# The SSD layer's in-chunk product of both directions as one product of the unscaled x, its decay matrix formed one pair ahead

## The chip, the cores and the metric

The kernel runs on one core of a Trainium2 chip. The metric is the time of the program on the device in microseconds (us), the median of the runs; lower is better. TensorE (PE) multiplies matrices, VectorE (DVE), ScalarE (ACT) and GpSimd (POOL) do elementwise work, SyncE (SP) issues the DMAs.

## The reference, cut to what matters

Two token groups (256 and 512 tokens, 768 in all) pass two layers with shared weights. Layer 0 is a bidirectional Mamba-2 SSD mixer with 32 heads of 64, in chunks of 128 tokens, layer 1 a neighbourhood attention. The change touches the SSD mixer only:

```python
def ssd_chunked(x, a_dt, bm, cm):
    ...
    decay_ls = jnp.exp(jnp.where(lower, seg, -jnp.inf))
    cb = jnp.einsum('bclgn,bcsgn->bcgls', cm, bm)
    y_diag = jnp.einsum('bcgrls,bcsgrp->bclgrp', cb[:, :, :, None] * decay_ls, x)
    ...
    return (y_diag + y_off).reshape(b, t, SSD_HEADS, p)

def ssd_direction(xs, bm, cm, dt_raw, dt_bias, a_log):
    dt = jax.nn.softplus(dt_raw.astype(jnp.float32) + dt_bias.astype(jnp.float32))
    ...
    return ssd_chunked(xs * dt[..., None].astype(xs.dtype), a_dt, bm, cm)
...
    y_fwd = ssd_direction(xs, bm, cm, dt_f, dt_bias_f, a_log_f)
    y_bwd = flip(ssd_direction(flip(xs), flip(bm), flip(cm), flip(dt_b), dt_bias_b, a_log_b))
    y = (y_fwd + y_bwd + d_skip[:, None] * xs)
```

So inside a chunk y is (C B masked to one triangle, times the decay) times (x dt_f), plus the same with the other triangle times (x dt_b). All is float32.

## The kernel before

Every engine has its own instruction list, written out by hand; semaphores order them. An engine runs its list strictly in order, so a wait holds up all that stands behind it.

`ssd_phase` goes through 16 pairs of heads (n = 0 to 15), for all 768 tokens (6 chunks of 128) at once. In pair n PE does, in this order:

- a dense unit, the input projection of x for pair n+1 (`pe_dense`, 24 products with 256 columns, then 24 with 512); between these two halves `turn_x` (L1791) transposes x of pair n;
- the chunk states (L1820), which need x scaled (`x_scaled`) and write over the banks A[2], A[3] in which the transposed x lay;
- the sums of squares of pair n-1 (L1797), in pairs 3, 7, 11 also the transposes for the next group of B (L1772);
- the dense unit of z for pair n; in "group pairs" 1, 5, 9 two more dense units, the next B and C;
- in pairs 3, 7, 11 C B of the next group (L1781);
- in even pairs from 2 on ("out pairs") two units of the output projection (`pe_out`, L264), 12 tiles, each of which DVE adds to `acc` (L298, copies at L296 in pair 2);
- the y block (L1850, L1854): per chunk two products for each direction with the in-chunk decay matrices `dec` and `seg` (L1850), and those with the carried states (L1854). It waits for `gated` of pair n-1, `carried`, `dec_ready` and `cs_ready`.

DVE in pair n: `scale_x` (L1631, from the turned x four products: with the two state weights and with dt_f and dt_b), in pairs 0, 4, 8, 12 the masked C B (L1649: `cb_u`, `cb_l`), the segment sums (L1656, L1659), the low part of the mix (L1618), C times the decays (L1674), then `dec` and `seg` from the exponentials and `cb_u`, `cb_l` (L1684, L1685), the carries (L1692), the convolution of x for pair n+1 (four taps, L1262; in out pairs they stand between the output tiles, the last one behind tile 10 of 12; in group pairs the taps of B and C follow), then waits for `y_done` and does y (L1732) and the gate (L1735).

ACT in pair n: exponentials (L1528, with a table load), the take of x for pair n+1 (L1200, L1201), the exponentials of the segments (`decay`, L1537, twelve of 128x128), the copies of the states (L1551 to L1553), the take of z (L245, L246), SiLU of the convolved x for pair n+1 (L1210, behind `conv_done`; in group pairs that of C comes last), then, behind `gated`, the square (L1573) and the high part of the mix (L1586), and so on with pair n+1.

POOL splits every weight unit in two (L188, L191). The names the change touches: `xx`/`xdt`/`xw`, `wt` (0, 1: state weights; 2, 3: dt_f, dt_b), `dec`, `seg`, `cb_u`, `cb_l`, `dec_ready`, `x_scaled`, `cb_taken`.

Of the kernel before, what the change touches and what calls it, by code (L numbers as in the profile page):

```python
# [14 lines left out]
P = 128  # L15
# [3 lines left out]
T = NP_ + NS  # L19
# [61 lines left out]
def encoder_kernel(nc, x_prompt, x_sample, mem_prompt, mem_sample, pre_g, post_g, mem_g, w_mem_kv, w_out,  # L81
# [3 lines left out]
    with ctx:  # L85
# [5 lines left out]
        def sem(name):  # L91
            return ctx.enter_context(nc.semaphore(name))
# [482 lines left out]
        def memory_phase(phase, L, pre=None, place=None, ssd=None):  # L575
# [32 lines left out]
            if L:  # L608
                with ExitStack() as after:
# [12 lines left out]
                sem(n + x) for x in ("post_gain_landed", "summed", "added", "post_sums", "post_root", "post_scaled",  # L622
                                     "x1_stored"))
            macc_landed, res_landed = ([sem(f"{n}{x}{i}") for i in range(2)] for x in ("macc_landed", "res_landed"))
# [472 lines left out]
        class Prelude:  # L1097
# [9 lines left out]
            def window(self, r):  # L1107

                at, r.at = r.at, 0
                self.ab, self.cs, self.xx = r(2, 2, T), r(2, 2, 4, P), r(4, NT, P)  # L1110
# [270 lines left out]
        def ssd_phase(phase, pre, nxt, mixes):  # L1381
            w_in = ssd_w_in[0]
            ab, cs, xx = pre.ab, pre.cs, pre.xx
            xw, xdt = xx[:, 0:2, :, :], xx[:, 2:4, :, :]
# [17 lines left out]
             expanded) = (  # L1402
# [3 lines left out]
                    "sq_done", "sq_summed", "summed", "reduced", "rooted", "expanded"))  # L1406
# [49 lines left out]
            def sync(sp):  # L1456
# [35 lines left out]
                sp.wait_ge(x_scaled, PAIRS)  # L1492
                nxt.load_mem(sp, 3)
# [10 lines left out]
            def scalar(act):  # L1504
                take_raw, silu = pre.takes(act)
                def take_bt(g):

                    act.wait_ge(bt_turned, g + 1)
                    if g:
                        act.wait_ge(states_done, 4 * g)  # L1510
                    act.activation(btok[:, 0:2, :], A[5][:, 0:NP_].rearrange("p (c l) -> p c l", l=P), ACT.Copy)
                    act.activation(btok[:, 2:6, :], A[4][:, :].rearrange("p (c l) -> p c l", l=P), ACT.Copy)\
                        .then_inc(bt_taken, 1)

# [3 lines left out]
                for n in range(PAIRS):  # L1518
# [23 lines left out]
                    if n < LAST:  # L1542
                        take_raw(j, n + 1)
# [54 lines left out]
            def vector(dve):  # L1598
# [13 lines left out]
                def both_heads(t):  # L1612
                    return t.unsqueeze(2).broadcast_to(shape)

# [8 lines left out]

                for n in range(PAIRS):
                    g, a = n // 4, n % 2
                    def scale_x():
                        dve.wait_ge(x_turned, n + 1)
                        for q, (c0, c1) in enumerate(((0, 2), (2, 6))):
                            ch = slice(2 * c0, 2 * c1)
                            pieces = [P, 4, 2 * (c1 - c0), 64]  # L1630
                            i = dve.tensor_tensor(  # L1631
                                xx.rearrange("p k c (h f) -> p k (c h) f", h=2)[:, :, ch, :],
                                A[2 + q][:, 0:(c1 - c0) * P].rearrange("p (c f) -> p c f", f=64).unsqueeze(1)
                                .broadcast_to(pieces),
                                wt[:, :, n, ch].unsqueeze(3).broadcast_to(pieces), ALU.mult)
# [7 lines left out]
                    if n % 4 == 0:  # L1643
# [8 lines left out]
                        dve.wait_ge(cb_taken, g + 1)  # L1652

# [28 lines left out]

                    dve.wait_ge(seg_exp, n + 1)
# [79 lines left out]
            def tensor(pe):  # L1763
                def chunk(bank2, ch):
                    return bank2[ch > 1][:, (ch if ch < 2 else ch - 2) * P:][:, 0:P]
# [37 lines left out]
                for n in range(PAIRS):  # L1803
# [12 lines left out]
                    pe.wait_ge(x_scaled, n + 1)  # L1816
                    pe.wait_ge(bt_taken, g + 1)
# [568 lines left out]
```

## Time and profile before

| | us |
|---|---|
| median of 3 runs | 2189.82 (2189.72 to 2192.56) |
| span of the profiled execution | 2187.1 |
| PE busy | 2125.7 (97%) |
| DVE busy | 1086.6 (50%) |
| ACT busy | 712.5 (33%) |
| POOL busy | 930.9 (43%) |

The span of the profiled execution is its own time as the profiler sees it; the median of the runs is 2.7 us above it. Columns of a page line and of a group of instructions: line and engine, operation, out<-in, count, then busy us and mean ns of one, then the idle time before them and what ended it. The SSD pairs run from 411 to 992 us of the span. Busy shares are of time in which at least one instruction was under way; a PE that is busy may still wait inside its pipeline.

### The profile page before, as it was taken

To read this page: it belongs to the slowest core of one execution; us is meant where nothing else is said; L and a number is where in the kernel's file an instruction comes from. 1 tells how busy PE (TensorE), PEld (TensorE's weight loads), DVE (VectorE), ACT (ScalarE), POOL (GpSimd) and SP (SyncE) were. 2 spreads that over 40 slices of the span, in tenths; PEclk is the share of its full clock that TensorE was granted. 3 is DMA by queue.
4 is the path that set the end of the run, shared out by engine and by line. 5 is a ranking of instruction groups with operands and counts; after the bars stand their busy time and mean duration, and the time that the engine had idled before them with its cause. 6 is when DMAs were issued, how large, how long until landed. Compare 5 with 4: busy or idle time off the path is not lost.

```text
span 2187.1 us, 31495 instructions
## 1 busy us (share of the span) xinstructions
PE 2125.7 (97%) x12986; PEld 1817.9 (83%) x12986; DVE 1086.6 (50%) x1685; ACT 712.5 (33%) x1618; POOL 930.9 (43%) x623
## 2 busy tenths in 40 slices
PE   7999999999999999999999999999999999999997
PEld 6888887888888888887788887888888888888885
DVE  4103333688888888897711333144323423541436
ACT  4123122344353344443322121043323323432243
POOL 4533333232443442334743333655454445554534
PEclk9999999999999999999999999999999999999999
DMA  6221212344322232334441111322231223122212
GB/s 193 87 70 51 53 55 81 116 105 113 97 94 80 78 106 78 96 106 155 136 135 49 49 58 39 104 85 62 62 87 57 67 57 94 43 64 85 66 49 116
DMA packets 206666, 184.72 MB, mean 84 GB/s; under 512 B 23899, under 2 KB 172667, under 8 KB 206523
## 3 DMA queue, kind: packets, MB, share of 16 engines
q1 hardware_dynamic: 206523, 182.72, 27.2%
q8 instruction: 102, 1.67, 0.3%
q14 instruction: 41, 0.34, 0.1%
HBM read 168.71 MB, written 12.21 MB: 83 GB/s over the span
## 4 chain that ended last, share of the span: by engine, by line
PE 49%; DVE 4%; issue 1%; ACT 1%; DMA 0%; POOL 0%; DVEq 0%; POOLq 0%
PE bank L214 24%; PE bank L264 9%; PE bank L567 6%; PE bank L2288 2%; PE bank L2259 2%; PE bank L2271 2%; PE bank L1000 2%; PE bank L1026 1%; DVE acc L911 1%; PE bank L1064 1%; DVE acc L915 1%; DVE acc L905 0%; PE bank L440 0%; DVE R L2148 0%; PE bank L2328 0%
## 5 line engine op out<-in xcount | busy, mean ns | idle before, releaser
L188 POOL TENSOR_SCALAR Wh<-Wraw 128x1024 fp32r<-128x1024 f32 x217 | 252.3, 1163 | 1137.9 <-issue 765.5
L214 PE MATMUL bank<-Hh,Wh 128*128 128x512 f32 (+1 forms) x1936 | 664.9, 343 | 6.3 <-ACT R L1201 3.6
L214 PE MATMUL bank<-Hl,Wh 128*128 128x512 f32 (+1 forms) x1936 | 652.2, 337 | 0.0
L214 PE MATMUL bank<-Hh,Wl 128*128 128x512 f32 (+1 forms) x1936 | 651.2, 336 | 0.0
L191 POOL TENSOR_TENSOR Wl<-Wraw,Wh 128x1024 fp32r<-128x1024 f32 x217 | 550.2, 2535 | 18.1
L214 PEld LDWEIGHTS bank<-Hh,Wh 128*128 128x128 f32 x1936 | 367.5, 190 | 54.8 <-issue 14.3
L214 PEld LDWEIGHTS bank<-Hh,Wl 128*128 128x128 f32 x1936 | 367.1, 190 | 38.9
L214 PEld LDWEIGHTS bank<-Hl,Wh 128*128 128x128 f32 x1936 | 367.7, 190 | 36.5 <-issue 1.7
L298 DVE TENSOR_TENSOR acc<-bank,acc 128x512 f32<-128x512 f32 x240 | 164.9, 691 | 170.6 <-PE bank L264 169.7
L264 PE MATMUL bank<-Wh,Mh 128*128 128x512 f32 x528 | 209.3, 396 | 11.3 <-DVE acc L298 11.3
L264 PE MATMUL bank<-Wh,Ml 128*128 128x512 f32 x528 | 206.5, 391 | 0.0
L264 PE MATMUL bank<-Wl,Mh 128*128 128x512 f32 x528 | 206.5, 391 | 0.0
L2025 POOL TENSOR_TENSOR R<-R 128x160 f32<-128x160 f32 (+2 forms) x160 | 109.1, 720 | 84.1 <-DVE R L2184 84.0
L1262 DVE SCALAR_TENSOR_TENSOR R<-R 128x770 f32<-128x770 f32 x96 | 135.8, 1420 | 13.2 <-ACT R L1201 11.7
L264 PEld LDWEIGHTS bank<-Wh,Mh 128*128 128x128 f32 x528 | 99.5, 189 | 38.9 <-DVE acc L298 17.2
L2157 DVE TENSOR_TENSOR R<-bank,R 128x256 f32<-128x256 f32 (+1 forms) x32 | 24.3, 837 | 206.5 <-PE bank L2288 206.5
L2148 DVE TENSOR_SCALAR R<-R 128x256 f32<-128x256 f32 (+2 forms) x192 | 126.2, 723 | 1.1
L931 DVE TENSOR_REDUCE R<-bank 128x2 f32<-128x512 f32 x24 | 16.6, 692 | 214.5 <-PE bank L1026 214.5
L2178 DVE CUSTOM_DVE_ANT_0 R<-bank,R 128x160 f32<-128x160 f32 (+2 forms) x192 | 57.9, 365 | 127.6 <-PE bank L2259 127.3
L264 PEld LDWEIGHTS bank<-Wl,Mh 128*128 128x128 f32 x528 | 99.6, 189 | 21.2
L264 PEld LDWEIGHTS bank<-Wh,Ml 128*128 128x128 f32 x528 | 99.5, 188 | 19.7
L246 ACT ACTIVATE R<-bank 128x512 f32<-128x512 f32 x62 | 37.1, 598 | 218.4 <-PE bank L214 218.4
(238 smaller groups left out, 3067.2 us busy)
## 6 DMA issues: line engine op xcount, KB each, us to landing
Wraw<-in_na_w_in_dram SPq DMA_DIRECT2D x80, 512.0 KB, 3.7
Wraw<-in_ssd_w_in_dram SPq DMA_DIRECT2D x57, 512.0 KB, 4.2
Wraw<-in_w_out_dram SPq DMA_DIRECT2D x48, 512.0 KB, 3.3
R<-acs_dram SPq DMA_DIRECT2D x16, 1536.0 KB, 6.2
Wraw<-in_w_mem_kv_dram SPq DMA_DIRECT2D x32, 512.0 KB, 3.7
R<-gs_dram SPq DMA_DIRECT2D x32, 128.0 KB, 3.5
macc_dram<-acc SPq DMA_DIRECT2D x1, 3072.0 KB, 9.1
R<-macc_dram SPq DMA_DIRECT2D x6, 512.0 KB, 4.2
```

Source lines behind the costliest of these rows:

```text
L188: pool.tensor_scalar(Wh[:, s, :], Wraw[:, s, :], 1.0, 1.0, ALU.mult, ALU.mult).then_inc(pool_c, 1)
L191: pool.tensor_tensor(Wl[:, s, :], Wraw[:, s, :], Wh[:, s, :].bitcast(F32), ALU.subtract)\
L214: mm = pe.matmul(DB[h.k % 2][:, 0:t1 - t0], w[:, k, :], x[:, k, t0:t1], start=(k == 0 and i == 0), stop=(k == KC - 1 and i == 2))
L264: mm = pe.matmul(A[4 + o.k % 2][:, :], x[k][:, i * P:(i + 1) * P], w[:, k, :], start=(k == 0 and j == 0), stop=(k == 1 and j == 2))
L298: dve.tensor_tensor(dst, A[4 + o.k % 2][:, :], dst, ALU.add).then_inc(out_added, 1)
L567: mm = pe.matmul(self.banks[t][:, :], x[:, 2 * j + k, tok], y[:, k, :], start=(j == 0 and k == 0 and p == 0), stop=(j == 3 and k == 1 and ...
L1000: mm = pe.matmul(V_BANK[t][:, :], x[:, 2 * j + k, tok], y[:, k, :], start=(j == 0 and k == 0 and p == 0), stop=(j == 3 and k == 1 and p == 2))
L1262: i = dve.scalar_tensor_tensor(o, x[:, k:k + w], self.cw[:, m + 24 * k:m + 24 * k + 1], o, ALU.mult, ALU.add)
L2025: i = pool.tensor_tensor(o, m, src, ALU.add)
L2148: i = dve.tensor_scalar(s, s, rinv[:, o, h:h + 1], None, ALU.mult)
L2178: i = dve.tensor_tensor_reduce(Sb[:, h, S_AT[b]:S_AT[b] + w], A[3 * h + bk][:, c0:c0 + w], Bm[:, h, m:m + w], 1.0, -3e38, ALU.add, ALU.max ...
L2259: mm = pe.matmul(A[3 * h + bk][:, c0:c0 + w], qF[f, q0:q0 + P], kF[f, k0:k0 + w], start=True, stop=True)
```

## The change

Since both in-chunk products of a head are summed, they can be one: with E the exponential of the segments, y = sum over s of x times E times (cb_u dt_f + cb_l dt_b). The new kernel

- forms that bracket M for pair n+1 at the end of pair n. ACT (`forward`) writes `dec` = cb_u * dt_f, twelve copies of 128x128 with a scale of one number per partition, behind its last SiLU of the pair and ahead of `gated`; DVE (`backward`) adds cb_l * dt_b with twelve scalar_tensor_tensor of 128x128, behind the last tap and ahead of `y_done`. Those of pair 0 stand in pair 0, ahead of `decay` and of the product with E;
- makes one product of E and M on DVE (`seg`) where there were two (L1684, L1685);
- halves the products of L1850 on PE: x unscaled (`xtok`) times `seg`, two per chunk instead of four;
- has DVE scale x with two weights instead of four (L1631), and ACT copy the unscaled x from PSUM (`copy_x`, 256 and 512 columns), behind `x_scaled` and between the two halves of the take of x for pair n+1; PE's states (L1820) wait for this copy too (`x_copied`);
- moves the masked C B of groups 1 to 3 from the start of pairs 4, 8, 12 to the end of pairs 3, 7, 11, ahead of `backward`;
- leaves out seven semaphores in layer 0 to have three new ones.

```diff
+                def copy_x(n):
+                    act.wait_ge(x_scaled, n + 1)
+                    for q, (c0, c1) in enumerate(((0, 2), (2, 6))):
+                        i = act.activation(xtok[:, c0:c1, :], A[2 + q][:, 0:(c1 - c0) * P]
+                                           .rearrange("p (c f) -> p c f", f=P), ACT.Copy)
+                    i.then_inc(x_copied, 1)
+
+                def forward(n):
+                    if n % 4 == 0:
+                        act.wait_ge(cb_taken, n // 4 + 1)
+                    if n:
+                        act.wait_ge(dec_ready, n)
+                    for ch in range(NT):
+                        for h in range(2):
+                            i = act.activation(dec[:, ch, h, :], cb_u[:, ch, :], ACT.Copy,
+                                               scale=wt[:, 2, n, 2 * ch + h:2 * ch + h + 1])
+                    i.then_inc(dec_forward, 1)
...
                     if n < LAST:
-                        take_raw(j, n + 1)
+                        take_raw(j, n + 1, lambda: copy_x(n))
+                    else:
+                        copy_x(n)
+                    if n == 0:
+                        forward(0)
                     decay()
...
                     elif n < LAST:
                         silu(j, n + 1, xs[1 - a])
+                    if n < LAST:
+                        forward(n + 1)
...
+                def backward(n):
+                    dve.wait_ge(dec_forward, n + 1)
+                    for ch in range(NT):
+                        for h in range(2):
+                            i = dve.scalar_tensor_tensor(dec[:, ch, h, :], cb_l[:, ch, :],
+                                                         wt[:, 3, n, 2 * ch + h:2 * ch + h + 1], dec[:, ch, h, :],
+                                                         ALU.mult, ALU.add)
+                    i.then_inc(dec_both, 1)
...
-                            pieces = [P, 4, 2 * (c1 - c0), 64]
+                            pieces = [P, 2, 2 * (c1 - c0), 64]
...
+                    if n == 0:
+                        backward(0)
                     dve.wait_ge(seg_exp, n + 1)
-                    c.add(dve.tensor_tensor(dec, seg, both_heads(cb_u), ALU.mult))
-                    dve.tensor_tensor(seg, seg, both_heads(cb_l), ALU.mult).then_inc(dec_ready, 1)
+                    dve.wait_ge(dec_both, n + 1)
+                    dve.tensor_tensor(seg, seg, dec, ALU.mult).then_inc(dec_ready, 1)
...
+                    if next_group(n):
+                        take_cb(g + 1)
+                    if n < LAST:
+                        backward(n + 1)
 
                     dve.wait_ge(y_done, n + 1)
...
                     pe.wait_ge(x_scaled, n + 1)
+                    pe.wait_ge(x_copied, n + 1)
...
-                        for d, weight in enumerate((dec, seg)):
-                            for h in range(2):
-                                pe.matmul(chunk(A[0:2], ch)[H64[h], :], xdt[:, d, ch, H64[h]], weight[:, ch, h, :],
-                                          start=(d == 0), stop=False)
+                        for h in range(2):
+                            pe.matmul(chunk(A[0:2], ch)[H64[h], :], xtok[:, ch, H64[h]], seg[:, ch, h, :],
+                                      start=True, stop=False)
```

## Rows read from the trace of the kernel before

**Rows 1.** Page, part 1: each engine's busy us, share and instructions.
```profile
PE 2125.7 (97%) x12986; PEld 1817.9 (83%) x12986; DVE 1086.6 (50%) x1685; ACT 712.5 (33%) x1618; POOL 930.9 (43%) x623
```
**Rows 2.** Windows by pair: length, busy PE, PEld, DVE, ACT, POOL, clock, DMA.
```profile
527.30:554.40 27.10, 27.10 (x230) 24.88 (x228) 24.50 (x26) 14.19 (x32) 6.46 (x4) 1.00 0.36 115
...
sum 580.80, PE 564.73 PEld 497.80 DVE 488.12 ACT 253.60 POOL 211.63; mean PE 35.30 PEld 31.11 DVE 30.51 ACT 15.85 POOL 13.23
```
**Rows 3.** Timeline of PE, end of pair 4 to states of pair 5.
```profile
592.98 0.66 PE L1850 MATMUL bank<-R 128*64 128x128 f32 x8
...
597.18 0.39 PE L1854 MATMUL bank<-R 128*64 128x128 f32 x4
...
606.61 1.95 PE L1820 MATMUL bank<-R 128*128 128x128 f32 x16
```
**Rows 4.** Timeline of DVE, same stretch: start, us, instruction, [idle before <-releaser].
```profile
592.34 1.01 DVE L1262 SCALAR_TENSOR_TENSOR R<-R 128x770 f32<-128x770 f32 x1
...
597.61 1.27 DVE L1732 SCALAR_TENSOR_TENSOR R<-R,bank 128x256 f32<-128x256 f32 x2 [3.67 <-PE bank L1854]
```
**Rows 5.** Timeline of ACT, same stretch, and its exponentials of the segments.
```profile
593.38 1.12 ACT L1210 ACTIVATE R<-R 128x256 f32<-128x256 f32 x2 [17.61 <-DVE R L1262]
599.91 0.85 ACT L1573 ACTIVATE R<-R 128x768 f32<-128x768 f32 x1 [5.40 <-DVE R L1735]
...
604.99 0.36 ACT L1200 ACTIVATE R<-bank 128x256 f32<-128x256 f32 x1
605.25 0.46 ACT L1201 ACTIVATE R<-bank,R 128x256 f32<-128x256 f32 x1
606.81 0.60 ACT L1200 ACTIVATE R<-bank 128x512 f32<-128x512 f32 x1 [1.10 <-PE bank L214]
...
610.37 3.63 ACT L1537 ACTIVATE R<-R 128x128 f32<-128x128 f32 x12 [2.38 <-DVE R L1659]
```
**Rows 6.** Timeline of DVE in pair 3: the removed forms, the nearest small ones.
```profile
539.30 2.49 DVE L1674 TENSOR_TENSOR R<-R 128x256 f32<-128x256 f32 x4
...
543.15 1.76 DVE L1684 TENSOR_TENSOR R<-R 128x1536 f32<-128x1536 f32 x1 [0.42 <-ACT R L1537]
...
546.50 1.75 DVE L1692 SCALAR_TENSOR_TENSOR R<-R,bank 128x64 f32<-128x64 f32 x8
```
**Rows 7.** Groups of DVE by form: the scaling of x, its two sizes.
```profile
L1631 DVE TENSOR_TENSOR R<-bank,R 128x2048 f32<-128x2048 f32 x16 | 36.5, 2280 | 0.0
L1631 DVE TENSOR_TENSOR R<-bank,R 128x1024 f32<-128x1024 f32 x16 | 19.6, 1223 | 12.1 <-PE bank L1791 11.9
```
**Rows 8.** Group pair 5, timelines: PE's y block starts; ACT's last SiLU.
```profile
636.26 0.66 PE L1850 MATMUL bank<-R 128*64 128x128 f32 x8
...
636.86 1.11 ACT L1210 ACTIVATE R<-R 128x256 f32<-128x256 f32 x2
```
**Rows 9.** Pair 3, timelines of DVE and PE: last taps, y, y block.
```profile
548.15 6.21 DVE L1262 SCALAR_TENSOR_TENSOR R<-R 128x770 f32<-128x770 f32 x3
554.53 1.26 DVE L1732 SCALAR_TENSOR_TENSOR R<-R,bank 128x256 f32<-128x256 f32 x2 [0.16 <-PE bank L1854]
...
549.89 0.66 PE L1850 MATMUL bank<-R 128*64 128x128 f32 x8
```
**Rows 10.** First pairs, timelines of PE and DVE: waits, the taps of x.
```profile
433.28 0.93 PE L1850 MATMUL bank<-R 128*64 128x128 f32 x8 [2.19 <-DVE R L1692]
...
451.06 2.05 PE L1820 MATMUL bank<-R 128*128 128x128 f32 x16 [0.95 <-DVE R L1631]
...
433.14 9.41 DVE L1262 SCALAR_TENSOR_TENSOR R<-R 128x770 f32<-128x770 f32 x4
```
**Rows 11.** Windows behind PE's wait of pair 0; the clock is third from last.
```profile
433.30:437.00 3.70, 3.70 (x38) 3.70 (x40) 3.67 (x2) 0.00 (x0) 3.62 (x3) 0.54 0.07 16
437.00:439.80 2.80, 2.80 (x48) 2.63 (x45) 2.73 (x3) 0.00 (x0) 2.72 (x2) 1.00 0.50 138
```
**Rows 12.** Waits of PE, whole span: us in total, times, longest.
```profile
PE bank L264 <- DVE acc L298: 13.4, 9, 2.8
```

More of the change, by code:

```diff
@@ L621, in memory_phase @@
             post_gain_landed, summed, added, post_sums, post_root, post_scaled, x1_stored = (
-                sem(n + x) for x in ("post_gain_landed", "summed", "added", "post_sums", "post_root", "post_scaled",
-                                     "x1_stored"))
-            macc_landed, res_landed = ([sem(f"{n}{x}{i}") for i in range(2)] for x in ("macc_landed", "res_landed"))
+                sem(n + x) if L else None for x in ("post_gain_landed", "summed", "added", "post_sums", "post_root",
+                                                    "post_scaled", "x1_stored"))
+            macc_landed, res_landed = ([sem(f"{n}{x}{i}") for i in range(2)] if L else None
+                                       for x in ("macc_landed", "res_landed"))
             where = InOrder() if L == 0 else ByColumn()
@@ L1109, in window @@
                 at, r.at = r.at, 0
-                self.ab, self.cs, self.xx = r(2, 2, T), r(2, 2, 4, P), r(4, NT, P)
+                self.ab, self.cs, self.xx = r(2, 2, T), r(2, 2, 4, P), r(3, NT, P)
                 r.at = at
@@ L1383, in ssd_phase @@
             ab, cs, xx = pre.ab, pre.cs, pre.xx
-            xw, xdt = xx[:, 0:2, :, :], xx[:, 2:4, :, :]
+            xw, xtok = xx[:, 0:2, :, :], xx[:, 2, :, :]
             raw, conv, bT, acs_tok, tot_tok, wt, cw, dcol, ssum = (
@@ L1401, in ssd_phase @@
              ab_exp, dec_ready, cs_ready, y_done, gated, hi_ready, sq_done, sq_summed, summed, reduced, rooted,
-             expanded) = (
+             expanded, x_copied, dec_forward, dec_both) = (
                 sem("g_" + x) for x in (
@@ L1405, in ssd_phase @@
                     "seg_ready", "seg_exp", "ab_exp", "dec_ready", "cs_ready", "y_done", "gated", "hi_ready",
-                    "sq_done", "sq_summed", "summed", "reduced", "rooted", "expanded"))
+                    "sq_done", "sq_summed", "summed", "reduced", "rooted", "expanded", "x_copied", "dec_forward",
+                    "dec_both"))
             F_DST, B_DST = (1, 3, 4, 5), (0, 2, 3, 4)
@@ L1492, in sync @@
                 sp.wait_ge(x_scaled, PAIRS)
+                sp.wait_ge(dec_both, PAIRS)
                 nxt.load_mem(sp, 3)
@@ L1629, in scale_x @@
                             ch = slice(2 * c0, 2 * c1)
-                            pieces = [P, 4, 2 * (c1 - c0), 64]
+                            pieces = [P, 2, 2 * (c1 - c0), 64]
                             i = dve.tensor_tensor(
-                                xx.rearrange("p k c (h f) -> p k (c h) f", h=2)[:, :, ch, :],
+                                xw.rearrange("p k c (h f) -> p k (c h) f", h=2)[:, :, ch, :],
                                 A[2 + q][:, 0:(c1 - c0) * P].rearrange("p (c f) -> p c f", f=64).unsqueeze(1)
                                 .broadcast_to(pieces),
-                                wt[:, :, n, ch].unsqueeze(3).broadcast_to(pieces), ALU.mult)
+                                wt[:, 0:2, n, ch].unsqueeze(3).broadcast_to(pieces), ALU.mult)
                             if q:
@@ L1642, in vector, with take_cb @@
                         scale_x()
-                    if n % 4 == 0:
+                    def take_cb(g):
                         dve.wait_ge(bc_done, g + 1)
@@ L1652, in vector @@
                         dve.wait_ge(cb_taken, g + 1)
+                    if n == 0:
+                        take_cb(0)
                     def segment():
@@ L1681, in vector @@
                         conv5(j, n + 1, dense, (0,))
+                    if n == 0:
+                        backward(0)
                     dve.wait_ge(seg_exp, n + 1)
-                    c.add(dve.tensor_tensor(dec, seg, both_heads(cb_u), ALU.mult))
-                    dve.tensor_tensor(seg, seg, both_heads(cb_l), ALU.mult).then_inc(dec_ready, 1)
+                    dve.wait_ge(dec_both, n + 1)
+                    dve.tensor_tensor(seg, seg, dec, ALU.mult).then_inc(dec_ready, 1)
                     dve.wait_ge(prev_set, n + 1)
```

2 lines of the change are left out of this document (removed).

## The prediction

> **What bounds the kernel now.** I read the page first: PE is busy 97% of the span [rows 1]. So a gain has to come out of PE's list, and a loss has to be a wait that PE doesn't have today. Next I read windows cut at the ends of the y blocks, one for each of the 16 pairs. Over all of them, 580.8 us, PE is busy 564.7, so it waits 16.1 us; in pair 3 it doesn't wait at all (27.1 of 27.1 us), with DVE busy for 24.5 [rows 2]. The reader is to see that DVE has little room in such a pair, and that the page's 50% for DVE is a mean over stages and says nothing of this one. Then I read the timelines of PE, DVE and ACT for one stretch, from the y block of pair 4 to the states of pair 5 [rows 3 to 5], since the change puts new work just where these three hand over to each other. The result is worked out there.
>
> **What PE gives up.** The y block of pair 4 starts at 592.98 and DVE takes y from 597.61; the last matmul group starts at 597.18 [rows 3, 4]. That is 4.5 us for 80 records (48 of L1850, two for each product, and 32 of L1854), in one unbroken stream. Half of L1850 goes, 24 records, 24/80 x 4.5 = 1.35 us. For 16 pairs that is **-21.6 us**. If the stream were bound by something other than its records it would be less, not under 0.
>
> **Where the new work stands.** I count from the start of the y block of pair 4 (592.98 = 0). DVE's last tap of the convolution ends at 593.35, +0.4 [rows 4]; ACT's SiLU, two instructions, ends at 594.50, +1.5 [rows 5]. Today both are then idle: DVE 3.67 us until y_done, ACT 5.40 us until the gate [rows 4, 5]. The change fills this with a chain, not with parallel work: `forward` stands behind SiLU on ACT, `backward` waits for it on DVE, and DVE's y and gate stand behind `backward`.
>
> - `forward`: twelve ACT instructions of 128x128 with one number per partition. The twelve exponentials of the segments have the same count, size and such an operand: 3.63 us [rows 5]. It ends at +5.2.
> - `backward`: twelve DVE instructions of 128x128, from no row directly. Upper bound: the eight carries (same operation, 64 columns) take 1.75 us, 0.21 each start to start; 64 more columns at about 1.1 ns (1.76 us for 1536 columns) give 0.28, so 3.4 us. Lower bound: the four products L1674 take 2.49 us for 2048 columns, which leaves 0.06 each beyond the columns, so 0.20 and 2.4 us [rows 6]. I take 2.9, the middle: the first has the same operation, the second all operands in SBUF as here. It ends at +8.1.
>
> The y block now ends at +3.2 (4.55 - 1.35), but DVE begins y at +8.1: **4.9 us after y_done** where it was at once.
>
> **What hangs on it.** PE doesn't wait for the gate of the last pair soon, but for the states it does, through x. Behind DVE's y (597.61) come the gate, ACT's square (599.91), the high part, the table load, the exponentials and the first half of the take of x, whose last instruction ends at 605.71 and lets the next one start some 0.1 earlier [rows 4, 5]. There `copy_x` now stands, 256 and 512 columns, 0.27 + 0.60 = 0.87 us by the takes L1200 [rows 5]: 8.9 us after DVE began y. PE wants to start the states 9.0 us after y_done (597.61 to 606.61) [rows 3, 4]. So the new wait `x_copied` alone would have been free by 0.1 us, and for just that reason all of the 4.9 us falls on PE: a wait of 4.8 us in the pair behind. PE has no other work in its list to put before it. Its cover, were it gone by another 1 us (ACT busy at the take), costs 1 us more in each pair.
>
> SP's next load of the segment sums waits for ACT's exponentials and for L1659, and the weights queue behind it; these come later by the same delay as PE does, so I put nothing on the weights. SP's last new wait, `dec_both`, is met long before.
>
> **The sum of the new waits.**
> - Behind out pairs (2, 4, ... 14): 7 x 4.8 = 33.6.
> - Behind group pairs (1, 5, 9): the chain starts with SiLU of C, which ends at 637.97, +1.7 [rows 8]; + 3.7 + 2.9 = +8.3, 5.1 after y_done; less the 0.1, 3 x 5.0 = 15.0.
> - Behind pairs 3, 7, 11, 13: here DVE's taps are the last thing. They ended at 554.36, 4.5 after the y block's start [rows 9]. DVE enters pair 3 4.9 late, PE 4.8 late; DVE saves half of the scaling, (2.28 + 1.22)/2 = 1.75 [rows 7], and one product of 1.76 [rows 6], 3.5 in all. So the taps end at +1.1. Then the masked C B, moved to here, 2 us by the L1674 row (three times ahead of `forward`), `forward` and `backward` to +9.7, 6.5 after y_done. That is 6.4 behind the 0.1 of cover for three of them and 4.4 to 5 for pair 13; DVE and POOL slow each other in places, which varies these. I take 6 x 4 = 24.
> - Behind pair 0: taps of x took 9.41 us and end at 442.55 [rows 10]. + 1.1 + 3.7 + 2.9, then the same 8.9: `x_copied` at 459.2, where the states started at 451.06 [rows 10]: 8.
> - In pair 0 `forward` stands ahead of the exponentials, on the path to the carries for which PE waits 2.19 us today [rows 10]: +3.6 on ACT, -3.5 on DVE and an overlap with PE's dense unit. I put 0, bounds -2 and +3.6.
>
> Together **+80.6 us**.
>
> **What goes with it.** Of PE's 16.1 us of waits today [rows 2], some lie where DVE or ACT was a little late: at the output tiles (13.4 us in the whole span, at nine places [rows 12]), at the states and at the takes. The new wait stands ahead of them in the same pair and takes their place. I put **-10**, bounds 0 and -14. The moved mask and shorter DVE list act only here.
>
> **The clock.** PE waited 2.19 us in pair 0, and then the granted clock was 0.54 for 3.7 us (1.2 GHz for most of it) and 1.00 after it [rows 10, 11]: 1.7 us lost. Each of the 15 new waits is longer than that one. Behind the waits of even pairs DVE and ACT don't set the next delay, PE's output tiles do, so the loss stays; before the others DVE is last and hides it. 7 x 1.7 = 12, bounds 0 and 15 x 1.7 = 26; I take **+10**. The Trainium skill ("TensorE: Matmul & The Clock Gate", "HAM oscillation") says that a wait that comes back in every trip of a loop pays the change of the clock each time; the row on pair 0 agrees for one wait. By that rule the sum would have the 26 in place of the 10.
>
> The Trainium skill ("VectorE: DVE Perf Modes", on the TRN2 errata) also speaks against this change: many small instructions from SBUF pay a fixed latency each, which one large one pays once. The rows show it mildly: twelve pieces are priced at 2.9 us here and the one product they stand for took 1.76. Its measured fixed term of about 150 cycles would make `backward` an estimated 3.5 us, and the sum some 9 us more.
>
> **Forecast.** -21.6 + 80.6 - 10 + 10 = **+59 us** on the span, 2187.1 to 2246. The median stands 2.7 above the span: 2189.8 + 59 = **2249 us**, 2.7% slower.
>
> **The rivals.**
> 1. *Half the chain is hidden.* If PE's states were released some 2.5 us earlier than I read (the takes and exponentials packed closer once they start late, or a `backward` under its bound), each of the 15 waits would be 2.5 shorter and the clock would mostly stay: 59 - 37 - 8 = +14, 2204. Against it: from y to the first take ACT has no idle gap to squeeze [rows 5]. 0.08.
> 2. *Faster, the other side.* PE's saving is kept whole if `backward` ends by y_done, that is if the chain behind the tap takes under 2.8 us (3.2 - 0.4) in place of 7.7. Then waits at the tiles shrink too: -21.6 - 3 = -25, 2165. For it: PE is the bound, and both DVE and ACT are idle just where the work is put. Against it: `forward` alone is 3.6 by its nearest row. 0.05.
> 3. *The clock falls each time and stays down longer.* If each wait costs 1.7 us of clock and more on the path (say 3, on all 15) and `backward` is at its upper bound (+0.5 each): 59 - 10 + 45 + 8 = +102, 2292. For it: the waits are twice as long as the one seen. Against it: DVE is last in every second pair and doesn't feel PE's clock. 0.12.
> 4. *The gain and the waits cancel* (within 4.4 us of before): needs the chain to be 3.4 us or so shorter; nothing points there. 0.02.
>
> The forecast has 0.73. Bounds inside it: `backward` 2.4 to 3.4 (-8, +8), the pairs 3, 7, 11, 13 from 5 to 7 each (-4, +4), clock -10 to +16, old waits -4 to +10, pair 0 +-3. These don't all go one way: -27 to +32, so 2222 to 2281; the 0.73 are nearly all in it. With a little of the third case the **range is 2220 to 2283**. A difference of 0.2% (4.4 us) is about what a measurement of this kernel tells from none. Faster 0.05, the same 0.02, slower 0.93.
>
> **What would show it.** In the profile after: y blocks of 3.2 us (right for the saving); PE's wait for L1820, released by ACT's copy from PSUM, 4 to 7 us in 15 pairs (right for the chain), with DVE idle between its last tap and the first small instruction for 4.5 to 5 us; a granted clock near 0.5 behind these waits. Wrong would be: PE waits only at y (then `dec` is last, not x), or `forward` found far from 3.6 us, or the states released by DVE rather than ACT, or no wait over 2 us in the out pairs.

## The result, and the profile after

The changed kernel takes 2291.97 us (median of 4 runs, 2288.70 to 2295.99) where the kernel before, run beside it, takes 2190.24: ratio 1.0463, 95% interval 1.0447 to 1.0479. That is 102 us slower; the prediction was 59 us slower, 2249, with a range up to 2283. The sign, the place and the length of the waits are as forecast; the price of TensorE's clock is not.

The page after: engines, and the granted clock in 40 slices of the span.

```profile
span 2291.9 us, 31139 instructions
...
PE 2163.0 (94%) x12602; PEld 1850.1 (81%) x12602; DVE 1063.3 (46%) x1861; ACT 780.2 (34%) x1842; POOL 919.3 (40%) x623
...
PEclk9999999988998899898999999999999999999999
```

PE has 384 records fewer than in [rows 1] (16 pairs x 24) and yet is busy 37 us longer. Fewer instructions and more busy time point to a slower clock, and slices 9 to 19, the SSD pairs, show it (before had 9 in every slice).

Windows cut at the ends of the y blocks (length, busy PE, PEld, DVE, ACT, POOL, clock, DMA), here pairs 1, 3 and 4:

```profile
438.70:498.50 59.80, 48.16 (x283) 42.77 (x283) 40.30 (x48) 27.36 (x65) 19.03 (x10) 0.83 0.34 88
...
549.80:584.70 34.90, 30.24 (x205) 27.69 (x206) 23.91 (x41) 18.90 (x46) 8.44 (x5) 0.85 0.28 91
...
584.70:632.70 48.00, 42.54 (x259) 36.50 (x259) 32.15 (x49) 19.32 (x49) 14.59 (x8) 0.93 0.24 77
```

Pair 3 was 27.10 us without a wait [rows 2]; it is 34.90 now, with PE idle for 4.66 and the rest a clock of 0.85. Over all 16 pairs the windows come to 682.20 us with PE busy 598.95, against 580.80 and 564.73 [rows 2]. So of the 101.4 us, **67.2 are idle PE** (83.25 in place of 16.07) **and 34.2 are busy PE**. Another 2.7 us lie ahead of the pairs, in work that the change doesn't touch, 0.7 behind them. The 2.7 are the clock of this execution: it was 0.51 from 16 to 23 us and 0.57 from 272 to 276 us, where the trace of before has 1.00. The traces of all thirteen runs start their first states at 419.1 to 423.5, whatever the kernel, and latest in the three in which the clock is down near 272 us.

The waits of PE in this stretch (us in total, times, longest):

```profile
PE bank L1864 <- issue: 63.9, 13, 5.5
PE bank L1864 <- DVE R L1665: 8.0, 1, 8.0
PE bank L1840 <- ACT R L1601: 6.1, 1, 6.1
PE bank L1834 <- ACT R L1211: 3.7, 1, 3.7
PE bank L1893 <- DVE R L1731: 1.6, 1, 1.6
```

L1864 are the states (L1820 before), which answer to [rows 3, 10]. There is one wait for each of pairs 1 to 14, as forecast; the one forecast for pair 15 stands at its sums of squares (L1840). "issue" says that the record names no releaser: the instruction waits for two semaphores. The timelines do name it. From the last tap of pair 4 to the states of pair 5, DVE and then ACT, the answer to [rows 4, 5]:

```profile
628.80 1.01 DVE L1263 SCALAR_TENSOR_TENSOR R<-R 128x770 f32<-128x770 f32 x1
...
634.52 3.24 DVE L1653 SCALAR_TENSOR_TENSOR R<-R 128x128 f32<-128x128 f32 x12 [4.10 <-ACT R L1533]
637.68 1.26 DVE L1775 SCALAR_TENSOR_TENSOR R<-R,bank 128x256 f32<-128x256 f32 x2
```
```profile
629.85 1.12 ACT L1211 ACTIVATE R<-R 128x256 f32<-128x256 f32 x2 [16.36 <-DVE R L1263]
630.88 3.61 ACT L1533 ACTIVATE R<-R 128x128 f32<-128x128 f32 x12
639.97 0.84 ACT L1601 ACTIVATE R<-R 128x768 f32<-128x768 f32 x1 [5.48 <-DVE R L1778]
...
645.67 0.87 ACT L1521 ACTIVATE R<-bank 128x256 f32<-128x256 f32 x2
```

Read them as one staircase: tap to 629.81, SiLU to 630.97, `forward` (L1533) to 634.49, `backward` (L1653) to 637.76, y, gate, square, exponentials, take, `copy_x` (L1521) to 646.54, and PE starts the states at 646.63. The y block had ended at 632.73; y starts 4.95 after it.

PE's states, some of the 15, with their idle time in brackets:

```profile
423.51 1.95 PE L1864 MATMUL bank<-R 128*128 128x128 f32 x16
461.35 3.75 PE L1864 MATMUL bank<-R 128*128 128x128 f32 x16 [7.96 <-DVE R L1665]
...
646.63 3.75 PE L1864 MATMUL bank<-R 128*128 128x128 f32 x16 [4.69 <-issue]
742.00 3.76 PE L1864 MATMUL bank<-R 128*128 128x128 f32 x16 [4.68 <-issue]
778.78 3.75 PE L1864 MATMUL bank<-R 128*128 128x128 f32 x16 [5.45 <-issue]
...
1012.61 3.60 PE L1864 MATMUL bank<-R 128*128 128x128 f32 x16 [4.68 <-issue]
```

The same 16 products take 1.95 us in pair 0 and 3.1 to 3.8 behind each wait. Windows behind the waits ahead of the states of pairs 3, 7 and 13, which were all of 4.66 to 4.68 us (length, busy PE, PEld, DVE, ACT, POOL, then the clock):

```profile
563.65:570.00 6.35, 6.35 (x30) 6.35 (x31) 5.95 (x7) 5.17 (x17) 0.00 (x0) 0.50 0.57 215
...
742.00:753.30 11.30, 11.30 (x53) 11.30 (x54) 10.80 (x18) 6.04 (x19) 1.45 (x1) 0.50 0.75 233
1012.61:1016.10 3.49, 3.49 (x18) 3.49 (x18) 3.49 (x5) 2.98 (x9) 0.00 (x0) 0.52 0.26 81
```

In the first PE is busy all 6.35 us at 1.2 GHz, so 3.2 us are lost there; the clock stays down until 572.4, and the whole stretch loses 4.4. In the second 5.6 are lost and in the third 1.7, though the waits ahead of them were equal. Over all 16 places it is 1.6 to 6.0 us each, 58 in all. In [rows 11] the clock was 0.54 for 3.7 us.

### The profile page after: what moved, and what is told of

Read it like the earlier page. It is cut to its first block, busy times and chain, and to the rows that moved or that the text cites. A ratio compares the mean times of both kernels' runs of the same rounds, so it can differ in the third digit from the quotient of the medians.

```text
span 2291.9 us, 31139 instructions
## 1 busy us (share of the span) xinstructions
PE 2163.0 (94%) x12602; PEld 1850.1 (81%) x12602; DVE 1063.3 (46%) x1861; ACT 780.2 (34%) x1842; POOL 919.3 (40%) x623
## 4 chain that ended last, share of the span: by engine, by line
PE 83%; DVE 9%; ACT 4%; issue 3%; DMA 1%; POOL 0%; SPq 0%; DVEq 0%; POOLq 0%
PE bank L214 43%; PE bank L264 15%; PE bank L567 6%; PE bank L1001 4%; PE bank L1864 2%; ACT R L1533 2%; PE bank L2314 2%; PE bank L2331 2%; PE bank L1027 2%; PE bank L2302 2%; DVE R L1653 1%; PE bank L1840 1%; PE bank L1065 1%; DVE R L1665 1%; PE bank L440 1%
## 5 line engine op out<-in xcount | busy, mean ns | idle before, releaser
L188 POOL TENSOR_SCALAR Wh<-Wraw 128x1024 fp32r<-128x1024 f32 x217 | 242.6, 1118 | 1254.4 <-issue 889.9
L214 PE MATMUL bank<-Hh,Wh 128*128 128x512 f32 (+1 forms) x1936 | 673.6, 348 | 2.6 <-ACT R L793 1.4
L214 PE MATMUL bank<-Hl,Wh 128*128 128x512 f32 (+1 forms) x1936 | 660.1, 341 | 0.0
L214 PE MATMUL bank<-Hh,Wl 128*128 128x512 f32 (+1 forms) x1936 | 657.9, 340 | 0.0
L191 POOL TENSOR_TENSOR Wl<-Wraw,Wh 128x1024 fp32r<-128x1024 f32 x217 | 548.4, 2527 | 18.1
L214 PEld LDWEIGHTS bank<-Hh,Wh 128*128 128x128 f32 x1936 | 375.9, 194 | 50.7 <-issue 9.9
L214 PEld LDWEIGHTS bank<-Hh,Wl 128*128 128x128 f32 x1936 | 374.8, 194 | 39.6
L214 PEld LDWEIGHTS bank<-Hl,Wh 128*128 128x128 f32 x1936 | 375.8, 194 | 36.8 <-issue 1.7
L1263 DVE SCALAR_TENSOR_TENSOR R<-R 128x770 f32<-128x770 f32 x96 | 124.0, 1291 | 31.4 <-ACT R L1202 29.9
L1864 PE MATMUL bank<-R 128*128 128x128 f32 x256 | 55.3, 404 | 71.8 <-issue 63.9
```

The source lines that it names most:

```text
L188: pool.tensor_scalar(Wh[:, s, :], Wraw[:, s, :], 1.0, 1.0, ALU.mult, ALU.mult).then_inc(pool_c, 1)
L191: pool.tensor_tensor(Wl[:, s, :], Wraw[:, s, :], Wh[:, s, :].bitcast(F32), ALU.subtract)\
L214: mm = pe.matmul(DB[h.k % 2][:, 0:t1 - t0], w[:, k, :], x[:, k, t0:t1], start=(k == 0 and i == 0), stop=(k == KC - 1 and i == 2))
L1263: i = dve.scalar_tensor_tensor(o, x[:, k:k + w], self.cw[:, m + 24 * k:m + 24 * k + 1], o, ALU.mult, ALU.add)
L1864: mm = pe.matmul(A[2 + d][:, s * P:(s + 1) * P], btok[:, src[s], :], xw[:, d, src[s], :], start=True, stop=True)
```

## The experiments

All times are medians beside runs of the kernel before on the same chip (2189.7 to 2190.4). "After" is the changed kernel.

### Is it the clock? Other products in the waits

**e5_warm_first** puts products that nobody reads into PE's list ahead of both waits:

```diff
+                    if n:
+                        pe.wait_ge(gated, n)
+                        for _ in range(34 if n == 1 else 20):
+                            pe.matmul(A[1][:, :], Hh[:, 0, 0:P], Hh[:, 0, NP_:T], start=True, stop=True)
                     pe.wait_ge(x_scaled, n + 1)
                     pe.wait_ge(x_copied, n + 1)
```

> As e1_warm (the kernel after with products that nothing reads), but these stand ahead of both waits, for the scaled and for the copied x, and there are 34 of them in pair 1. In e1 PE sat 2.7 us idle for the scaled x before it came to them in every second pair, and then did 4.8 us of them, past the moment when x was there. Here they fill the idle time itself. Theory A (the clock costs some 50 us on top of the waits): 2236 to 2248. Theory B (it doesn't): 2285 to 2295.

Measured: 2250.84 us, ratio 1.0277 (1.0259 to 1.0296), 3 us above the range of theory A and far from theory B. The kernel is 41 us faster than after, with more work on PE. In its trace the states take 2.02 us wherever they come behind such products, with what is left of the waits:

```profile
751.09 2.02 PE L1868 MATMUL bank<-R 128*128 128x128 f32 x16 [0.92 <-issue]
...
994.71 2.02 PE L1868 MATMUL bank<-R 128*128 128x128 f32 x16 [1.28 <-issue]
```

So at least 41 of the 102 us are clock; the waits themselves are still paid, by products instead of idleness. Two waits have no such cover, and the clock still falls behind them: at `turn_x` in pair 1 (3.6) and at the sums of squares in pair 15 (6.1).

**e1_warm** has the same 20 products between the two waits, so PE stands idle for `x_scaled` first.

```diff
                     pe.wait_ge(x_scaled, n + 1)
+                    if n:
+                        pe.wait_ge(gated, n)
+                        for _ in range(20):
+                            pe.matmul(A[1][:, :], Hh[:, 0, 0:P], Hh[:, 0, NP_:T], start=True, stop=True)
                     pe.wait_ge(x_copied, n + 1)
```

> The kernel after, with 20 products of 128x512 that nothing reads (4.6 us at full clock) put on PE ahead of its wait for the copied x, in pairs 1 to 15. The waits there are 4.7 to 8 us, so the products lie inside them and only keep PE busy. Theory A (about 55 us of the 101 lost in the SSD pairs are the lower clock behind 15 waits, not the waits): the clock stays near 1.00, 2292 falls by 45 to 52 to 2240 to 2247, although PE has more work. Theory B (what comes on top of the waits is late data or shared ports, and the low clock only goes with it): no gain, 2290 to 2300.

Measured: 2275.16, ratio 1.0387 (1.0366 to 1.0408), between the two. The reason is in its waits and two of its blocks:

```profile
PE bank L1863 <- DVE R L1665: 24.4, 10, 6.4
```
```profile
552.75 6.42 PE L1863 MATMUL bank<-Hh 128*128 128x512 f32 x20 [2.73 <-DVE R L1665]
585.53 4.83 PE L1863 MATMUL bank<-Hh 128*128 128x512 f32 x20 [0.57 <-DVE R L1665]
```

In six pairs PE stands idle for 2.7 us first, and then the products run on past the time at which `x_copied` is given (`copy_x` ends at 554.61, the products at 559.17), so the chain gets longer. Behind five of the six waits the clock fell as well, so that the products themselves took 6.4 to 6.5 us in place of 4.83; behind the sixth, of 2.71, it stayed. The states come at the full clock (1.95 to 2.05 us) each time. The run mixes all this; e5 is the one that prices the clock.

### Is it where the new work stands? The same change without "a step ahead"

**e2_own_pair** keeps everything of the change (one product with the bracket, half of PE's in-chunk products, `copy_x`), but forms M of pair n in pair n: `forward` ahead of `decay`, `backward` ahead of the product, the masked C B back at pairs 4, 8, 12.

```diff
+            EARLY = ()
...
-                    if n == 0:
-                        forward(0)
+                    if n not in EARLY:
+                        forward(n)
                     decay()
...
-                    if n < LAST:
-                        forward(n + 1)
...
-                    if n == 0:
-                        take_cb(0)
+                    if n % 4 == 0:
+                        take_cb(g)
...
-                    if n == 0:
-                        backward(0)
+                    if n not in EARLY:
+                        backward(n)
                     dve.wait_ge(seg_exp, n + 1)
...
-                    if next_group(n):
-                        take_cb(g + 1)
-                    if n < LAST:
-                        backward(n + 1)
```

> The kernel after, but M of pair n is formed in pair n: ACT's twelve copies behind the take of x and ahead of the exponentials of the segments, DVE's twelve ahead of the product with E; the masked C B at the start of pairs 4, 8, 12 as before. The same instructions, only elsewhere. Theory A (it is the place, behind SiLU and ahead of the gate, that costs): no waits of 4 to 8 us are left, PE keeps its 21.6 us less some 4 for the wait on the copied x behind odd pairs: 2172 (2163 to 2182). Theory C (it is the load, 24 small instructions a pair on engines without room): DVE becomes last in pairs without output tiles, 2190 to 2210.

Measured: 2179.83 us, ratio 0.9956 (0.9940 to 0.9972); again on another chip:

> The same program as e2_own_pair, run again beside the two behind it so that the three share a chip. Expected: 2178 to 2182 us again, 0.4 to 0.5% under the kernel before.

Measured: 2179.89, ratio 0.9952 (0.9938 to 0.9965). So the change without the step ahead is a gain of 10 us, and the step ahead (M and the masked C B together) costs 112. Its waits of PE in the pairs (the second run):

```profile
PE bank L1888 <- DVE R L1730: 6.6, 2, 5.0
PE bank L1829 <- ACT R L1211: 6.3, 3, 3.7
PE bank L1859 <- issue: 5.0, 3, 1.9
PE bank L214 <- ACT R L1202: 3.2, 3, 1.3
PE bank L264 <- DVE acc L298: 2.8, 3, 1.4
```

The 14 long waits at the states are gone (three are left, at `copy_x`, 1.9 at most). One long one has come: 5.0 at the y block of pair 15.

**e10_last_forward** is e2_own_pair with something done about that one alone: `AHEAD` holds pair 15.

```diff
-                    if n not in EARLY:
+                    if n not in AHEAD:
                         forward(n)
                     decay()
...
                     act.activation(prev[:, 1, 3, :], A[3][:, 3 * P:4 * P], ACT.Copy).then_inc(prev_set, 1)
+                    if n + 1 in AHEAD:
+                        forward(n + 1)
```

> e2_own_pair with forward of the last pair alone issued one step ahead on ACT, behind the copies of the states of pair 14; backward and the product stay in pair 15. In e2_own_pair PE waits 5.0 us at the y block of pair 15 for DVE's carries. Theory (the wait comes from ACT doing forward, 3.6 us, in front of the exponentials of the segments there, with no other work to cover it): the wait falls to about 1.4 us, total 2175 to 2178. Rival (it comes from DVE's own additional work, backward 3.2 us less what was saved, so ACT's order does not matter): the wait stays at 4 to 5 us and the total within 1 us of e2_own_pair.

Measured: **2172.57 us**, ratio 0.9930 (0.9918 to 0.9943), 7.3 under e2b_own_pair (4.9 by the means, since two of the five runs of e10 are at 2177): more than expected. The y block of pair 15 and the clock behind its wait (third from last) in e2b_own_pair and then here:

```profile
977.34 0.69 PE L1888 MATMUL bank<-R 128*64 128x128 f32 x4 [5.00 <-DVE R L1730]
...
977.34:981.00 3.66, 3.66 (x37) 3.66 (x39) 2.02 (x3) 3.52 (x7) 1.26 (x2) 0.53 0.76 284
```
```profile
971.18 0.44 PE L1891 MATMUL bank<-R 128*64 128x128 f32 x4 [1.73 <-DVE R L1733]
...
971.18:975.00 3.82, 3.82 (x59) 3.55 (x60) 2.47 (x4) 3.67 (x6) 0.18 (x1) 1.00 1.00 340
```

The wait is 3.3 us shorter, and the clock that fell behind the long one (1.7 us lost) stays up behind the short one: 5.0 us together. The two traces are 7.9 us apart, but of that 2.2 lie ahead of the pairs, which the edit doesn't touch, so the rest of the 7.3 can't be put down to this wait. With e11, below, this is the fastest kernel of this study.

**e11_odd_forward** is the same with `AHEAD` holding the pairs 1, 3, 5, 7, 9, 11, 13, 14 and 15.

> e2_own_pair with forward issued one step ahead on ACT, behind the copies of the states, for pairs 1, 3, 5, 7, 9, 11, 13, 14 and 15; backward stays in its own pair in front of the product. Theory (a part moved ahead is free where its engine waits anyway and nobody's list stands behind it; ACT waits 2 to 4 us at this place): no new waits of PE; the remaining waits at turn_x, 7.1 us in five places, shrink by 0 to 3 us with the one of pair 15, total 2172 to 2177. Rival (moving it ahead delays the exponentials and SiLU that stand behind it on ACT, as every step moved ahead did so far): new waits of 1 to 2 us in the pairs concerned, total 2183 to 2195.

Measured: 2172.66, ratio 0.9922 (0.9909 to 0.9934), no different from e10. So there is no sign of the rival, and of the theory only what pair 15 brings. Its waits at `turn_x` are 5.1 us in four places in place of 6.6 in four, those at `copy_x` 5.4 in place of 4.3. `forward` on ACT can be moved here for nothing, and brings nothing beyond pair 15.

### Which link of the chain?

**e9_forward_early** is after, with `forward` issued behind the copies of the states in the pairs 1, 2, 4, 5, 6, 8, 9, 10, 12, 13 and 14; `backward` stays where the change put it.

```diff
+                    if 0 < n < LAST and not next_group(n):
+                        forward(n + 1)
                     if group_unit(n):
                         take_raw(j + 1, g + 17)
...
-                    if n < LAST:
+                    if next_group(n) or n == 0:
                         forward(n + 1)
```

> The kernel after with one move: ACT's twelve copies stand behind those of the states (pairs 1, 2, 4, 5, 6, 8, 9, 10, 12, 13, 14), 10 us before the last tap; in pairs 0, 3, 7, 11 and for DVE's twelve pieces all is as in the kernel after. The chain behind the tap is 3.6 + 1.1 us shorter in eleven pairs, so DVE can begin with backward at once: the waits there of 4.7 to 5 us go to 0.3 or so. Theory A with the clock: 11 x (4.6 + 3.3) = 87 less, 2205. Without the clock (only waits go): 2241. Theory C (the load of small instructions): hardly a change.

Measured: 2250.42, ratio 1.0276 (1.0257 to 1.0294); 41.5 less than after, half of the 87 that the shorter chain should have brought. The waits behind out pairs are 2.90, not 0.3. `backward` in the trace, and POOL at the same time:

```profile
534.09 5.64 DVE L1655 SCALAR_TENSOR_TENSOR R<-R 128x128 f32<-128x128 f32 x12
...
569.61 3.24 DVE L1655 SCALAR_TENSOR_TENSOR R<-R 128x128 f32<-128x128 f32 x12 [3.76 <-ACT R L1533]
```
```profile
533.46 1.05 POOL L188 TENSOR_SCALAR Wh<-Wraw 128x1024 fp32r<-128x1024 f32 x1 [4.80 <-issue]
534.59 2.36 POOL L191 TENSOR_TENSOR Wl<-Wraw,Wh 128x1024 fp32r<-128x1024 f32 x1
```

`backward` is 2.40 us longer, and POOL's L191, which runs inside it, takes 2.36. In all six places behind out pairs it is 5.64 to 5.66, with an L191 inside, and in the five where no L191 runs at the same time it is 3.24. In after it is 3.24 in all 16, and no L191 falls into any of them. The wait that went had kept two engines apart. The states behind the six waits of 2.90 still have the low clock (3.33 to 3.65):

```profile
630.86 3.65 PE L1866 MATMUL bank<-R 128*128 128x128 f32 x16 [2.90 <-issue]
```

**e4_one_backward** is after with one of the twelve instructions of `backward`; the other eleven pieces of the backward term are left out.

```diff
-                    for ch in range(NT):
-                        for h in range(2):
+                    for ch in range(1):
+                        for h in range(1):
```

> The kernel after with one of the twelve DVE pieces that add cb_l dt_b; the other eleven are left out, so M lacks that term in eleven of twelve tiles. The chain is 3.0 us shorter in 15 pairs, waits of 1.7 to 2.5 us in place of 4.7 to 5.5. Theory A with a clock that falls only behind waits of some 2 us and more: 45 us of waiting and most of the 55 of clock go, 2195 to 2205. If the clock's loss is in proportion to the wait: 45 and about 30 go, 2217. If nothing of it is the clock: 2247.

Measured: 2208.16, ratio 1.0081 (1.0061 to 1.0101): 84 us less than after, for eleven instructions of 0.27 us in each pair (3.0 us, 48 for 16 pairs). PE's waits in the pairs are 41 us shorter (84.3 to 43.6), and the other 43 are busy PE, since the clock stays up behind eleven of the fourteen waits ahead of the states:

```profile
455.53 3.75 PE L1864 MATMUL bank<-R 128*128 128x128 f32 x16 [4.74 <-issue]
545.12 2.02 PE L1864 MATMUL bank<-R 128*128 128x128 f32 x16 [1.80 <-issue]
...
888.60 2.02 PE L1864 MATMUL bank<-R 128*128 128x128 f32 x16 [2.56 <-issue]
```

Three of the waits are of 2.56 us. Behind two of them the states took 2.02, behind the third, at 573.73, 3.65: at this length both happen. Behind one of 2.92 they took 2.59.

**e3_gaps** forms M a step ahead for the pairs 3, 5, 7, 9, 11, 13 and 15 only, and takes `backward` apart: one of its instructions (two in pair 14) behind each output tile. The rest is as in e2_own_pair.

```diff
-                            dve_out(dve, (half,), first=(n == 2), then=lambda k: tap(j, n + 1, 2 * half + k) if n < LAST else None)
+                            for tile in range(NT):
+                                dve_out_tiles(dve, half, (tile,), lambda k: tap(j, n + 1, 2 * half + k), n == 2)
+                                backward(n + 1, (NT * half + tile,))
```

> As e2, but for pairs 3, 5, ... 15 M is formed one pair ahead in true gaps: ACT's copies behind those of the states, where ACT then waits over 10 us for the taps, DVE's twelve one by one behind the output tiles, at each of which it waits some 0.2 to 0.8 us. Theory A: not slower than e2, 2168 (2160 to 2180), since the pairs with little room on DVE are relieved. Theory C: each small piece delays the next tile by 0.27 us, 7 x 12 x 0.27 = 23 us more than e2.

Measured: 2192.92, ratio 1.0008 (0.9998 to 1.0017), 13 us more than e2_own_pair. In the traces PE is idle 9.8 us longer than in e2b_own_pair over the whole run (77.1 against 67.3) and busy 3.1 longer. One line has grown most:

```profile
PE bank L264 <- DVE acc L298: 19.2, 27, 1.4
```

DVE looks idle between tiles, but PE waits for the tiles there: 27 short waits, where e2b_own_pair has 3 (2.8 us); other waits, the one of 5.0 among them, have shrunk.

### What the parts are worth alone

**e7_half_products** is the kernel before with the forward half of the in-chunk products only; the backward term is left out, all work of DVE and ACT stays.

```diff
-                        for d, weight in enumerate((dec, seg)):
+                        for d, weight in enumerate((dec,)):
```

> The kernel before with only the forward half of the in-chunk products on PE (12 of 24 in each pair; the backward term is left out of y), everything else as it was. It measures by itself what PE gives up. If the saving of 1.35 us a pair is kept: 2190 less 21.6 is 2169. If DVE is last in the pairs without output tiles, so that PE only waits longer for it there (pairs 0, 3, 7, 11, 13, 15): 6 to 8 us of it are lost, 2175 to 2177.

Measured: 2182.27, ratio 0.9965 (0.9953 to 0.9977): 8 us, not 21.6. Its waits of PE in the pairs and just behind them:

```profile
PE bank L264 <- DVE acc L298: 12.3, 7, 2.8
PE bank L1791 <- ACT R L1210: 4.2, 2, 3.6
PE bank L1850 <- DVE R L1692: 3.7, 2, 2.2
```

Before has 8.2 us at the tiles in the same stretch and 1.2 at `turn_x`. A faster PE comes earlier to places where DVE or ACT was just in time. Over the whole run PE is idle 67.3 us in place of 61.4 and busy 12.6 less in place of 21: the clock is down in more places, such as 0.57 from 581 to 585 us behind a wait of 2.81 at an output tile. Some of it lies ahead of the pairs, which start 2.7 us late as in after, with the clock at 0.57 from 270 to 278 us.

**e6_copy_first** is e2_own_pair with `copy_x` moved ahead of the exponentials for C (`decays_of_c`, four instructions) in the pairs 1 to 14, to be rid of the wait at `copy_x`.

```diff
+                    def copy_and_decays():
+                        copy_x(n)
+                        decays_of_c()
+
+                    if n in (0, LAST):
+                        decays_of_c()
...
-                        take_raw(j, n + 1, lambda: copy_x(n))
+                        take_raw(j, n + 1, copy_and_decays if n else lambda: copy_x(n))
```

> As e2_own_pair, but in pairs 1 to 14 ACT copies x before it takes the exponentials for C (with their table load), 3.5 us earlier. e2 has three waits of 1.3 us at the states of pairs 4, 8, 12 for that copy. If those are all that it costs, 3 to 5 us less than e2: 2175 to 2177. If the later exponentials hold up DVE's L1711 in the pairs without output tiles, the same as e2 or up to 5 us more.

Measured: 2190.08, ratio 1.0003 (0.9994 to 1.0012), 10 us more than e2_own_pair. The wait at the states is down to 0.3 us in all, and three others have grown:

```profile
PE bank L1837 <- ACT R L1211: 10.1, 5, 3.5
PE bank L1896 <- DVE R L1738: 9.0, 3, 5.0
PE bank L264 <- DVE acc L298: 8.6, 6, 2.6
PE bank L214 <- ACT R L1202: 4.3, 6, 1.2
```

The exponentials release DVE's C times decays, and with them all of DVE's list. So this place of `copy_x` is worse than the one that the change has. Adding `copy_x` alone to the kernel before wasn't tried: `xtok` has no place beside four weighted copies of x.

## Why the prediction was right or wrong

**PE's saving (-21.6).** Right. The y block of pair 4 runs from 629.45 to 632.73, 3.28 us; before, from its first product to the end of its last, it was 4.59 (the 4.55 of the prediction reads the end a little early): -1.31 a pair, -21.0 in all. That most of it is gained as soon as the waits are gone is shown by e10_last_forward (-17), and that much of it is lost again in the old order of DVE and ACT by e7_half_products (-8).

**The chain (+4.9 after y_done).** Right in each link: forecast +0.4, +1.5, +5.2, +8.1 from the start of the y block; measured +0.4, +1.5, +5.0, +8.3. `forward` took 3.61 (priced 3.63), `copy_x` 0.87 (0.87), `backward` 3.24 (2.9, in its bounds of 2.4 to 3.4). The Trainium skill's fixed term ("VectorE: DVE Perf Modes", on the TRN2 errata) had given an estimated 3.5; the trace lies between the two, a little nearer to it.

**The new waits (+80.6).** Measured 78.0 in 15 places: behind pairs 2, 4, ... 12 4.66 to 4.69 (4.8), behind group pairs 4.86 to 4.87 (5.0), behind 3, 7 and 11 5.45 to 5.46 and behind 13 4.87 (6 each), behind pair 0 7.96 (8). The one behind pair 14 stands at the sums of squares, 6.14 (4.8). Pair 0's own `forward`, put at 0, cost nothing: DVE's taps start 11.8 us behind the start of the states there, 12.3 before. In 3, 7 and 11 the number holds but not the path. I had DVE's taps last; DVE is long done with them and waits for PE:

```profile
572.16 3.79 DVE L1263 SCALAR_TENSOR_TENSOR R<-R 128x770 f32<-128x770 f32 x3
581.48 0.42 DVE L1683 TENSOR_TENSOR R<-bank,mask_u 128x256 f32<-128x256 f32 x1 [5.53 <-PE bank L1824]
```

The moved mask needs C B (L1824), which PE does last before the y block. The masks, `forward` and `backward` so start with the y block whatever DVE does.

**The old waits (-10).** Right. Measured: 83.25 idle less 78.0 leaves 5.3 of 16.07, so -10.8. Most of the 5.3 is one wait of 3.69 at `turn_x` of pair 1, where before had 1.16. It isn't the new work's: e7_half_products, which has none of it, waits 3.59 there. PE comes earlier, since its y block of pair 0 takes 3.28 in place of 6.26 us.

**The clock (+10).** This is the step that failed. The terms above come to 78.0 - 10.8 - 21.0 = +46.2; the pairs grew by 101.4, and the 55.2 between them are TensorE at 1.2 GHz (the 58 us counted from the granted clock, less the 1.7 that before paid in pair 0, agree to within a microsecond or so). Both factors of "7 x 1.7" were too small.

- The price of one: 1.7 us came from the one wait of 2.19 in [rows 10, 11]. Behind the waits of after 55.2 / 16 = 3.5 are lost on the mean, but from 1.6 to 6.0 in single places: of the six waits of 4.66 to 4.69 us one cost 1.7, one 2.1 and one 5.6. No run here shows what decides it.
- The count: I said that behind the waits of odd pairs DVE is last and hides it. With 3.5 us less to do and a start that is late with PE's, it no longer is: in pair 3 it is busy for 23.91 of 34.90 us and waits for PE's C B. PE's clock is paid in all 16 places, behind the 15 new waits and behind the one at `turn_x`.

My third rival had both (1.7 us of clock and more on the path, say 3, on all 15) and gave 2292, the time measured. The agreement to the microsecond is luck: it also had `backward` at its upper bound (+8 us, measured 3.24, for some 5), and its 45 us of clock were 55. I gave it 0.12 since [rows 2] show DVE last in pair 3. That row was of the kernel before; the change itself took DVE off that path. The Trainium skill ("TensorE: Matmul & The Clock Gate", "HAM oscillation") has it that such a wait in a loop is paid with the clock each time; the trace of after agrees in 16 of 16 places, and the 26 that I had by its rule from the short wait are still half of what was measured. In e4_one_backward waits of 1.80 to 1.99 us came back in nine pairs and the clock stayed up.

What rows show of a wait ahead of the 16 state products, and of their time:

| idle PE | states | where |
|---|---|---|
| none | 1.95 | pair 0, all kernels |
| 0.9 to 2.0 | 2.02 (2.05 once) | before, e2b, e4, e5, e9 |
| 2.56 | 2.02, 2.02, 3.65 | e4, three |
| 2.90 | 3.33 to 3.65 | e9, six |
| 2.92 | 2.59 | e4, once |
| 3.69 | 2.54 | e9, once |
| 4.66 to 7.96 | 3.13 to 3.76 | after, e4, e9 |

What remains open: why the clock stays down for 3.5 us behind one wait and for over 11 behind its equal, and why some waits of the same length leave it up.

## What to carry to other kernels

Moving work a step ahead is free only where it ends no one's list: ask what stands behind it on each engine and who waits for that, and follow the chain to the next thing that PE needs; time in which two engines are both idle before a handover isn't free if the new work runs on them one after the other. Price a new wait of PE as its length plus the clock, from several waits of that length, since equal ones cost from 1.7 to 5.6 us here, and ask of every stage that "hides" the loss whether it is still last once the change is in. Before giving up a change, put the same work back into its own step: here that turned +102 us into -10, and one instruction group moved in the last pair made it -17.

## What the hardware showed that was not expected

- Filling PE's idle time with products that nobody reads made the kernel 41 us faster (2292.0 to 2250.8) though PE got its data no earlier for it: the products only took the place of idleness.
- Ahead of the state products no wait of up to 2.0 us was followed by 1.2 GHz, and each of 4.66 us and more was. Between them both happened: of three waits of 2.56 one was, and at `turn_x` of pair 1, behind a wait of 3.50 us, the clock stayed at 1.00 in e6_copy_first and was 0.67 for the next 5.2 us in e10_last_forward. The length of the wait alone doesn't tell: behind the pairs the clock of before fell to 0.50 for 3.8 us behind a wait of 1.39 at an output tile, and at the start of its run, from 5 to 16 us, it stayed at 1.00 behind one of 9.29.
- DVE lost the time in which POOL worked on two operands from SBUF: twelve instructions of 3.24 us together took 5.64 with one POOL instruction of 2.36 inside, which is at the short end of what that line takes here (2.35 to 3.74). The Trainium skill ("SBUF — State Buffer", "SBUF: two separate sides") says that the two share ports that one of them holds for a whole instruction; these rows agree.
